# Projection of a hybrid diffusion layer: its token columns in four groups of 428 to 512 instead of six of 304

## The chip, the cores and the metric

The kernel runs on one core of a Trainium2 chip. The metric is the device time of one execution in microseconds (us), the median of the runs. A core has a matmul engine (PE; its weight loads are shown apart as PEld), a vector engine (DVE), a scalar engine (ACT), a general engine (POOL), and SP, which here only issues DMA transfers. Each engine works through its own list of instructions in order, and they meet through semaphores.

## The reference, cut to what matters

One layer of a diffusion model over 1280 tokens (256 context tokens, 1024 latent ones), each with 1024 features, in float32. The part that is changed is the first:

```python
m = jax.nn.silu(cond) @ w_ada + b_ada          # modulation: 6 x 1024 columns, for two conditions
h = rmsnorm(x, gain) * (1.0 + scale) + shift   # adaln
gq, gk, gv, gg, glr, sq, sk, sv = jnp.split(h @ w_in, idx, axis=-1)   # 2848 columns
g_f = heads(jax.nn.log_sigmoid(lr_f @ w_gk_f + b_gk_f) / GATE_TEMP)   # gates, and g_b alike
```

After it come gated linear attention in both directions, windowed attention, the output projection and a squared-ReLU MLP, which the change leaves as they are. The 2848 columns of `w_in` are: 0 to 1023 the queries and keys of the linear attention, 1024 to 1535 its values, 1536 to 2047 an output gate, 2048 to 2079 the low-rank gate input, 2080 to 2847 query, key and value of the windowed attention.

## The kernel before, in words

A product in float32 is made of three matmuls on operands that are split in two, `x = hi + lo`: hi·hi, hi·lo and lo·hi. `project` (L643) computes `h @ w_in`. It goes over the columns of `w_in` in groups (`GROUPS`, L351). Of a token group (columns from 1024 on) the items are the ten tiles of 128 tokens: 24 matmuls each (8 blocks of the contraction, three products), the token tile as the stationary operand and the weight columns, 304 of them, as the moving one. Of a channel group (queries and keys, 256 columns) the items are blocks of 128 columns times three chunks of 512, 512 and 256 tokens: the weights are stationary and the tokens move. That is 84 items in all, numbered n = 0 to 83. All engines run through the same item numbers and do, at fixed numbers, what is due there:

- PE multiplies item n into one of four PSUM banks, after the bank's last item has been copied out (`staged`). At a group's first item it waits for the group's split weights.
- ACT (odd n) or DVE (even n) copies item n to `stage`. SP stores it at position n and waits there until the copy is made (L725 and the line before it), so that everything SP issues later in its list waits too.
- A group's weights are loaded by SP into one of two rooms of `raw` at `FIRST_ITEM[g]` for group g + 1 (L377), split by ACT (high part, L814) and POOL (low part, L868) at item 2 or 3 of group g. The second group alone is split in halves, by DVE and POOL.
- The other two thirds of the modulation weights, 16 slices of 1 MB, use the same rooms after a group is split: SP loads one (L152), PE multiplies it (L188) at an item of `slice_at`, and its room may then be loaded again (`slice_used`).
- The gates (`Gates`, eight blocks, begun every 7 items): PE logits, ACT a softplus of seven instructions with two table loads (L594 to L598), DVE sums and a scan (L609 to L640), SP a store. The heads (`HeadsPrep`, ten tiles, begun every 4.5 items) norm and rotate the windowed queries and keys, in turns between POOL (L446 to L464) and DVE (L471 to L489).
- Near the end SP loads the keys and first tiles of the next stage.

An ACT position is, in order: copy out item n, split, softplus. A DVE position is: copy out item n, low part of a split (if any), modulation, gates, heads.

Of the kernel before, what the change touches and what calls it, by code (L numbers as in the profile page):

```python
# [108 lines left out]
class Modulation:  # L109
# [531 lines left out]
def project(nc, keep, a, raw, hi, lo, scratch, outs, keys, rec, room, stored, mod_out):  # L643
# [4 lines left out]
    with ExitStack() as ctx:  # L648
        s = Space(nc, ctx, "prj")
        whi = [s.sb(f"whi{j}", [P, KD, COLS_IN], F32R) for j in range(2)]  # L650
        wlo = [s.sb(f"wlo{j}", [P, KD, COLS_IN], F32R) for j in range(2)]
# [4 lines left out]
        whi_half, wlo_half, whi_ready, wlo_ready, first_lo_ready, acc_ready = (s.sem(n) for n in (  # L656
            "whi_half", "wlo_half", "whi_ready", "wlo_ready", "first_lo_ready", "acc_ready"))
# [26 lines left out]
        rows_at = {FIRST_ITEM[6]: 1, FIRST_ITEM[9] + 5: 2}  # L684
# [26 lines left out]
        with nc.Block() as block:  # L711
# [152 lines left out]
            def _(pool):  # L864
# [2459 lines left out]
```

## Time and profile before

| | |
|---|---|
| median of 3 runs | 1648.76 us (1645.47 to 1649.05) |
| the profiled execution | 1647.43 us, of which span 1645.7 us |
| mean granted TensorE clock | 0.991 |
| PE busy, share of the span | 1588.2 us, 97% |
| PEld, POOL, DVE, ACT busy | 85%, 62%, 59%, 42% |
| projection: first to last matmul | 40.2 to 388.4 us |

PE is busy in 97% of the span, and no other engine is near it. The page counts overlapping matmuls, so that busy time says nothing about how fast they follow each other: that is to be read from the starts of consecutive matmuls in the timeline. The profile covers one execution; 1.7 us of its time lie outside the span.

### The profile page before, as it was taken

What the parts mean: (1) busy time and instruction counts of PE and PEld (TensorE: products, weight loads), DVE (VectorE), ACT (ScalarE), POOL (GpSimd) and SP (SyncE); (2) the same over time, 40 slices, a digit from 0 to 9 for tenths busy, and PEclk for the clock granted to TensorE, in tenths of its full rate; (3) what the DMA queues carried; (4) which work ended last, traced back from release to release, by engine and by line L of the source; (5) the groups of instructions that cost most, each with busy time, mean ns of one, the idle gap of its engine ahead of it and who ended that gap; (6) DMA issues with size and microseconds to landing.
All of it is one profiled execution on the core that took longest, in us unless ns stands there. A gap on an engine that the chain in (4) does not pass through costs nothing.

```text
span 1645.7 us, 31938 instructions
## 1 busy us (share of the span) xinstructions
PE 1588.2 (97%) x11618; PEld 1391.1 (85%) x11618; DVE 973.5 (59%) x1503; ACT 687.3 (42%) x1212; POOL 1019.1 (62%) x784
## 2 busy tenths in 40 slices
PE   4999999998999999999999999999999999999998
PEld 1999778897788877788889899998979899998987
DVE  2713564775665665457866656666694545545468
ACT  2513323324454566213444444444535444444441
POOL 1711455573485799103777777687898767676673
PEclk7999999999999999999999999999999999999999
DMA  8344555749655763334743132331344132231313
GB/s 323 109 131 165 187 181 191 264 143 257 195 162 171 230 179 114 147 130 155 215 167 103 51 102 63 90 95 58 103 132 150 52 102 73 80 102 51 102 52 115
DMA packets 211450, 225.93 MB, mean 137 GB/s; under 512 B 52752, under 2 KB 171664, under 8 KB 208144
## 3 DMA queue, kind: packets, MB, share of 16 engines
q1 hardware_dynamic: 209248, 224.46, 42.9%
q8 instruction: 70, 1.15, 0.3%
q10 hardware_dynamic: 2096, 0.02, 0.1%
q14 instruction: 36, 0.29, 0.1%
HBM read 177.22 MB, written 47.24 MB: 136 GB/s over the span
## 4 chain that ended last, share of the span: by engine, by line
PE 44%; POOL 4%; DVE 1%; issue 1%; ACT 0%; DMA 0%; SPq 0%; DVEq 0%; ACTq 0%; POOLq 0%
PE ff_banks L3189 8%; PE ff_banks L3190 8%; PE ff_banks L3191 8%; PE ff_banks L3162 7%; PE ff_banks L3164 7%; PE ff_banks L3163 7%; POOL h_whi L2835 1%; POOL h_xop L2432 1%; POOL h_wlo L2847 1%; POOL h_whi L2842 1%; DVE ff_tmp L3036 0%; DMA ff_hb<-in_w_ff 0%; DVE ff_acc L3026 0%; DVE ff_acc L2993 0%; POOL h_wlo L2882 0%
## 5 line engine op out<-in xcount | busy, mean ns | idle before, releaser
L3162 PE MATMUL ff_banks<-h_xop,h_whi 128*128 128x320 f32 x888 | 275.2, 310 | 4.6 <-POOL h_whi L2835 2.0
L3164 PE MATMUL ff_banks<-h_xop,h_whi 128*128 128x320 f32 x888 | 274.4, 309 | 0.0
L3163 PE MATMUL ff_banks<-h_xop,h_whi 128*128 128x320 f32 x888 | 274.3, 309 | 0.0
L2993 DVE TENSOR_TENSOR ff_acc<-ff_acc,ff_banks 128x512 f32<-128x512 f32 x296 | 200.6, 681 | 100.5 <-PE ff_banks L3191 98.9
L3189 PE MATMUL ff_banks<-h_wlo 128*128 128x512 f32 x580 | 226.5, 390 | 1.6 <-POOL h_whi L2842 0.8
L3191 PE MATMUL ff_banks<-h_wlo 128*128 128x512 f32 x580 | 225.6, 389 | 0.0
L2835 POOL TENSOR_TENSOR h_whi<-mid_raw,h_whi 128x512 fp32r<-128x512 f32 x149 | 208.4, 1415 | 1.4 <-ACT h_whi L2687 1.4
L2847 POOL TENSOR_TENSOR h_wlo<-mid_raw,h_wlo 128x320 fp32r<-128x320 f32 x128 | 116.7, 913 | 127.4 <-ACT mid_raw L2724 127.4
L3162 PEld LDWEIGHTS ff_banks<-h_xop,h_whi 128*128 128x128 f32 x888 | 166.7, 188 | 8.3 <-issue 3.6
L3163 PEld LDWEIGHTS ff_banks<-h_xop,h_whi 128*128 128x128 f32 x888 | 166.7, 188 | 1.1
L3164 PEld LDWEIGHTS ff_banks<-h_xop,h_whi 128*128 128x128 f32 x888 | 166.7, 188 | 0.0
L972 PE MATMUL prj_banks<-prj_whi,h_hi 128*128 128x304 f32 x480 | 148.1, 309 | 3.4 <-DVE h_lo L341 2.2
L2835 POOL TENSOR_TENSOR h_whi<-ff_tmp,h_whi 128x512 fp32r<-128x512 f32 x63 | 105.6, 1676 | 67.6 <-ACT h_whi L2687 67.6
L974 PE MATMUL prj_banks<-prj_whi,h_lo 128*128 128x304 f32 x480 | 145.5, 303 | 0.0
L973 PE MATMUL prj_banks<-prj_wlo,h_hi 128*128 128x304 f32 x480 | 144.9, 302 | 0.0
L2687 ACT ACTIVATE h_whi<-mid_raw 128x512 fp32r<-128x512 f32 x149 | 89.9, 623 | 97.7 <-DVE mid_raw L2949 91.4
L3189 PEld LDWEIGHTS ff_banks<-h_wlo 128*128 128x128 f32 x580 | 108.9, 188 | 25.0 <-DVE ff_acc L2993 1.9
L3191 PEld LDWEIGHTS ff_banks<-h_wlo 128*128 128x128 f32 x580 | 108.9, 188 | 23.0
L2717 ACT ACTIVATE mid_raw<-wo_raw 128x320 f32<-128x320 f32 x128 | 60.3, 471 | 159.5 <-DVE wo_raw L2971 65.2
L3190 PE MATMUL ff_banks<-h_whi,h_wlo 128*128 128x512 f32 x310 | 120.7, 389 | 0.0
L3190 PE MATMUL ff_banks<-h_wlo 128*128 128x512 f32 x290 | 113.1, 390 | 0.0
L825 ACT ACTIVATE prj_stage<-prj_banks 128x304 f32<-128x304 f32 (+2 forms) x47 | 21.0, 446 | 220.5 <-PE prj_banks L974 133.7
(323 smaller groups left out, 3771.6 us busy)
## 6 DMA issues: line engine op xcount, KB each, us to landing
mid_raw<-in_w_ff SPq DMA_DIRECT2D x124, 512.0 KB, 4.4
mid_raw<-in_w_ada SPq DMA_DIRECT2D x18, 1024.0 KB, 7.2
early_room<-qk_by_channel SPq DMA_DIRECT2D x20, 512.0 KB, 4.2
proj<-prj_stage SPq DMA_DIRECT2D x60, 152.0 KB, 1.9
mid_raw<-in_w_in SPq DMA_DIRECT2D x6, 1216.0 KB, 7.3
early_room<-in_w_ada SPq DMA_DIRECT2D x6, 1024.0 KB, 11.1
decays<-early_room SPq DMA_DIRECT2D x8, 640.0 KB, 4.6
early_room<-decays SPq DMA_DIRECT2D x20, 256.0 KB, 2.9
```

Source lines behind the costliest of these rows:

```text
L972: pe.matmul(out, x_hi, whi[j][:, k, 0:w], start=(k == 0), stop=False)
L973: pe.matmul(out, x_hi, wlo[j][:, k, 0:w], start=False, stop=False)
L974: mm = pe.matmul(out, x_lo, whi[j][:, k, 0:w], start=False, stop=(k == KD - 1))
L2835: pool.tensor_tensor(lo, source(q, i), hi.bitcast(F32), ALU.subtract).then_inc(w1lo_ready, 1)
L2847: pool.tensor_tensor(ulo[j][c][:, t0:t0 + TH], v[i % 2], uhi[j][c][:, t0:t0 + TH].bitcast(F32), ALU.subtract).then_inc(ulo_ready, 1)
L2993: dve.tensor_tensor(acc[:, p, at], acc[:, p, at], down[n % RING], ALU.add).then_inc(added, 1)
L3162: pe.matmul(out, w_hi[:, k], x_hi[:, k], start=(k == 0), stop=False)
L3163: pe.matmul(out, w_hi[:, k], x_lo[:, k], start=False, stop=False)
L3164: mm = pe.matmul(out, w_lo[:, k], x_hi[:, k], start=False, stop=(k == KH - 1))
L3189: pe.matmul(out, x_hi, w_hi[c][:, at], start=(c == 0), stop=False)
L3190: pe.matmul(out, x_hi, w_lo[c][:, at], start=False, stop=False)
L3191: mm = pe.matmul(out, x_lo, w_hi[c][:, at], start=False, stop=(c == 1))
```

## The change

Token columns come in groups of 428, 428, 512 and 456 (1824 as before); the channel columns in groups of 256, 256, 128, 128 and 256. Group order: 428, 256, 428, 256, 512, 128, 128, 256, 456. There are 64 items instead of 84: 40 token items and the same 24 channel items; the groups begin at items 0, 10, 16, 26, 32, 42, 45, 48 and 54 (before: 0, 10, 20, 30, 36, 42, 48, 54, 64 and 74). The two rooms of `raw` get different sizes (8 x 512 and 8 x 256 words); `raw` and the split buffers grow by 15 KB per partition together, and a scratch area of the DMA is cut to 1024 bytes. All groups after the first are split in halves of the contraction: ACT makes both high halves, DVE the first low half and POOL the second. The numbers at which loads, splits, slices, gates and heads are due are written out as tables, in part closer together: gates now every 4 or 5 items and heads every 3 or 4, and two of a gate's steps on DVE one item earlier. The last group is loaded at item 47 and split by ACT at item 48, and slices are multiplied after items 49, 51 and 53.

The diff, cut to its core:

```diff
-GROUPS = ((1936, 304), (2240, 304), (2544, 304), (0, 256), (256, 256), (512, 256), (768, 256), (1024, 304), (1328, 304), (1632, 304))
+GROUPS = ((1992, 428), (0, 256), (2420, 428), (256, 256), (1024, 512), (512, 128), (640, 128), (768, 256), (1536, 456))
 NG = len(GROUPS)
-COLS_IN = max(w for _, w in GROUPS)
+COLS_IN = [max(w for _, w in GROUPS[j::2]) for j in range(2)]
+RAW_IN = [0, KD * COLS_IN[0], KD * sum(COLS_IN)]
 QK = 2 * GW
...
+def raw_group(raw, g):
+
+    at = RAW_IN[g % 2]
+    return raw[:, at:at + KD * GROUPS[g][1]].rearrange("p (k n) -> p k n", k=KD)
+
+
+def load_group(eng, a, raw, g):
     at, w = GROUPS[g]
-    return eng.dma_start(raw[:, j, :, 0:w], a["w_in"][0].rearrange("(k p) n -> p k n", p=P)[:, :, at:at + w])
+    return eng.dma_start(raw_group(raw, g), a["w_in"][0].rearrange("(k p) n -> p k n", p=P)[:, :, at:at + w])
...
-        turn_at = {FIRST_ITEM[1] + 5 + 2 * c: c for c in range(len(CHUNKS))}
-        gate_at = {FIRST_ITEM[2] + 7 * n: n for n in range(H)}
-        heads_at = {FIRST_ITEM[3] + 3 + 9 * t // 2: t for t in range(NT)}
-        assert max(gate_at) + 8 < LAST and max(heads_at) + 6 < LAST
-
-
-        slices = [(g, at) for g, places in ((2, (3, 7)), (3, (2, 5)), (4, (2, 5)), (5, (2, 5)), (6, (5,)), (7, (2, 5, 9)), (8, (1, 5, 9)), (9, (4,))) for at in places]
-        slice_at = {FIRST_ITEM[g] + at: i for i, (g, at) in enumerate(slices)}
-        slice_load_at = {}
-        for i, (g, at) in enumerate(slices):
-            same = i and slices[i - 1][0] == g
-            slice_load_at[FIRST_ITEM[g] + (slices[i - 1][1] + 1 if same else 0 if g < 7 else -1 if g == 7 else -3)] = i
+        turn_at = {15: 0, 17: 1, 19: 2}
+        gate_at = {20: 0, 24: 1, 29: 2, 33: 3, 38: 4, 42: 5, 47: 6, 51: 7}
+        heads_at = {22: 0, 25: 1, 29: 2, 33: 3, 36: 4, 40: 5, 43: 6, 47: 7, 51: 8, 54: 9}
+        load_at = {10: 2, 16: 3, 26: 4, 32: 5, 42: 6, 43: 7, 47: 8}
+        high_at = {12: 2, 19: 3, 28: 4, 35: 5, 42: 6, 44: 7, 48: 8}
+        low_at = [{13: 2, 21: 3, 29: 4, 36: 5, 42: 6, 45: 7, 50: 8}, {13: 2, 20: 3, 28: 4, 36: 5, 42: 6, 45: 7, 49: 8}]
+        TAIL = 60
+        assert len(ITEMS) == 64 and max(gate_at) + 6 < TAIL and max(heads_at) + 4 < TAIL
+
+
+        slices = [(2, 21), (2, 23), (2, 25), (3, 27), (3, 29), (4, 33), (4, 35), (4, 37), (4, 41), (5, 42), (7, 49), (7, 51), (7, 53), (8, 54), (8, 56), (8, 58)]
+        slice_at = {at: i for i, (g, at) in enumerate(slices)}
+        slice_load_at = {at: i for i, at in enumerate((17, 22, 24, 25, 28, 32, 34, 36, 38, 40, 48, 50, 52, 53, 55, 57))}
...
-        rows_at = {FIRST_ITEM[6]: 1, FIRST_ITEM[9] + 5: 2}
-        cols_at = {FIRST_ITEM[6] + 1: 1, FIRST_ITEM[9] + 6: 2}
-        pick_at = {FIRST_ITEM[6] + 2: 1, FIRST_ITEM[9] + 7: 2}
-        assert len(slices) == 2 * KD and slices[KD - 1][0] == 5 and slices[KD] == (6, 5)
+        rows_at = {38: 1, 59: 2}
+        cols_at = {39: 1, 60: 2}
+        pick_at = {40: 1, 61: 2}
+        assert len(slices) == 2 * KD and all(FIRST_ITEM[g] <= at < FIRST_ITEM[g + 1] for g, at in slices)
...
+        def half_of(g, half):
+
+            ks = slice(half * KH, (half + 1) * KH)
+            return raw_group(raw, g)[:, ks], wide(whi, g)[:, ks], wide(wlo, g)[:, ks]
+
+        def split_until(eng, g):
+
+            if g == 0:
+                eng.wait_ge(first_lo_ready, 1)
+            else:
+                for half in range(2):
+                    eng.wait_ge(wlo_ready[half], g)
+
+        def low_half(eng, g, half):
+
+            src, hi_out, lo_out = half_of(g, half)
+            eng.wait_ge(whi_ready[half], g)
+            eng.tensor_tensor(lo_out, src, hi_out.bitcast(F32), ALU.subtract).then_inc(wlo_ready[half], 1)
         def width(n):
...
-                    if n == FIRST_ITEM[g] and 1 <= g < NG - 1:
-                        if g == 1:
-                            sp.wait_ge(first_lo_ready, 1)
-                        else:
-                            sp.wait_ge(wlo_ready, g - 1)
-                        if used_until[g - 1]:
-                            sp.wait_ge(ada.slice_used, KD + used_until[g - 1])
-                        load_group(sp, a, raw, g + 1, (g + 1) % 2).then_inc(w_in[(g + 1) % 2], 16)
+                    if n in load_at:
+                        g = load_at[n]
+                        split_until(sp, g - 2)
+                        if used_until[g - 2]:
+                            sp.wait_ge(ada.slice_used, KD + used_until[g - 2])
+                        load_group(sp, a, raw, g).then_inc(w_in[g % 2], 16)
                     if n in slice_load_at:
                         i = slice_load_at[n]
                         room = slices[i][0]
-                        sp.wait_ge(wlo_ready, room)
-                        sp.wait_ge(ada.slice_used, KD + (i if room == g else used_until[room - 2]))
+                        split_until(sp, room)
+                        sp.wait_ge(ada.slice_used, KD + (i if slices[i - 1][0] == room else used_until[room - 2]))
...
-                    if n - 8 in gate_at:
-                        gates.sp_store(sp, gate_at[n - 8])
-                    if n == FIRST_ITEM[9]:
-                        sp.wait_ge(ada.slice_used, KD + used_until[8])
+                    if n - 6 in gate_at:
+                        gates.sp_store(sp, gate_at[n - 6])
+                    if n == FIRST_ITEM[NG - 1]:
+                        split_until(sp, NG - 1)
+                        sp.wait_ge(ada.slice_used, KD + used_until[NG - 2])
                         keys.sp_load_cache(sp)
-                    if n == max(heads_at) + 6:
-                        sp.wait_ge(ada.slice_used, 3 * KD)
+                    if n == TAIL:
                         for j in range(2):
...
+                def high_half(g, half):
+                    src, hi_out, lo_out = half_of(g, half)
+                    act.wait_ge(w_in[g % 2], 16 * (g // 2 + 1))
                     if g >= 2:
                         act.wait_ge(acc_ready, FIRST_ITEM[g - 1])
-                    act.activation(whi[j][:, :, cols], raw[:, j, :, cols], ACT.Copy).then_inc(whi_ready, 1)
-
-                def split_second(half):
-                    cols, ks = split_slices(1), slice(half * KH, (half + 1) * KH)
-                    act.wait_ge(w_in[1], 16)
-                    act.activation(whi[1][:, ks, cols], raw[:, 1, ks, cols], ACT.Copy).then_inc((whi_half, whi_ready)[half], 1)
+                    act.activation(hi_out, src, ACT.Copy).then_inc(whi_ready[half], 1)
...
-                    if n == FIRST_ITEM[g] + (2 if by_channel(g) else 3) and 1 <= g < NG - 1:
-                        split(g + 1)
+                    if n in high_at:
+                        for half in range(2):
+                            high_half(high_at[n], half)
...
-                    if n == FIRST_ITEM[g] + (2 if by_channel(g) else 3) and 1 <= g < NG - 1:
-                        split(g + 1)
+                        low_half(pool, 1, 1)
+                    if n in low_at[1]:
...
+                    if n in low_at[0]:
+                        low_half(dve, low_at[0][n], 0)
...
+                    if n - 3 in gate_at:
+                        gates.dve_gate(dve, gate_at[n - 3])
                     if n - 4 in gate_at:
-                        gates.dve_gate(dve, gate_at[n - 4])
+                        gates.dve_scan(dve, gate_at[n - 4])
                     if n - 5 in gate_at:
-                        gates.dve_scan(dve, gate_at[n - 5])
-                    if n - 6 in gate_at:
-                        gates.dve_relative(dve, gate_at[n - 6])
+                        gates.dve_relative(dve, gate_at[n - 5])
...
-        wide, late = PAST // P * KV * 2 * DH, NT * KV * 2 * DH
-        self.kc = flat[:, 0:wide].rearrange("p (b k c d) -> p b k c d", k=KV, c=2, d=DH)
-        self.k = flat[:, wide:wide + late].rearrange("p (t k c d) -> p t k c d", k=KV, c=2, d=DH)
+        at, late, wide = 4 * HALF, NT * KV * 2 * DH, PAST // P * KV * 2 * DH
+        self.k = raw[:, at:at + late].rearrange("p (t k c d) -> p t k c d", k=KV, c=2, d=DH)
+        self.kc = raw[:, at + late:at + late + wide].rearrange("p (b k c d) -> p b k c d", k=KV, c=2, d=DH)
...
-    nc = bacc.Bacc("TRN2", target_bir_lowering=False, num_devices=1)
+    nc = bacc.Bacc("TRN2", target_bir_lowering=False, num_devices=1, dynamic_dma_scratch_size=1024)
```

## Rows read from the trace of the kernel before

**Rows 1.** Waits of PE from 40 to 388.3 us, then busy time of 60 to 390:

```profile
PE prj_banks L972 <- DVE h_lo L341: 2.2, 1, 2.2
PE prj_banks L972 <- POOL h_lo L341: 1.2, 1, 1.2
PE prj_banks L188 <- DMA mid_raw<-in_w_ada: 0.3, 1, 0.3
...
60.00:390.00 330.00, 328.04 (x2125) 294.09 (x2123) 167.91 (x206) 98.21 (x121) 143.81 (x89) 1.00 0.56 176
```

**Rows 2.** Timeline of PE: start, duration, line; two matmuls 24 apart, two 15 apart:

```profile
100.01 0.30 PE L972 MATMUL prj_banks<-prj_whi,h_hi 128*128 128x304 f32 x1
...
103.35 0.30 PE L972 MATMUL prj_banks<-prj_whi,h_hi 128*128 128x304 f32 x1
...
160.02 0.40 PE L982 MATMUL prj_banks<-h_hi,prj_whi 128*128 128x512 f32 x1
...
163.50 0.39 PE L982 MATMUL prj_banks<-h_hi,prj_whi 128*128 128x512 f32 x1
```

**Rows 3.** Timeline of the start, and the window 22 to 34 us:

```profile
34.45 1.94 PE L188 MATMUL prj_banks<-mid_raw,prj_ada_silu 128*32 128x512 f32 x8
...
40.23 0.59 PE L972 MATMUL prj_banks<-prj_whi,h_hi 128*128 128x304 f32 x1 [2.24 <-DVE h_lo L341]
...
22.00:34.00 12.00, 5.95 (x31) 1.69 (x32) 4.96 (x4) 3.85 (x7) 4.00 (x6) 0.64 1.02 411
```

**Rows 4.** Timeline of DVE and POOL, 293 to 305 us, and a scan:

```profile
293.70 0.83 DVE L478 SCALAR_TENSOR_TENSOR prj_xn<-early_room,prj_rstd 128x640 f32<-128x640 f32 x1 [0.26 <-POOL prj_rstd L452]
...
296.39 2.35 POOL L464 TENSOR_TENSOR prj_sq<-prj_xg,prj_rope 128x320 f32<-128x320 f32 x2
298.70 5.40 POOL L868 TENSOR_TENSOR prj_wlo<-mid_raw,prj_whi 128x2432 fp32r<-128x2432 f32 x1
...
298.83 5.96 DVE L489 TENSOR_TENSOR prj_xr<-prj_xc,prj_sq 128x640 f32<-128x640 f32 x1 [1.66 <-POOL prj_sq L464]
...
339.85 2.83 DVE L621 TENSOR_TENSOR_SCAN early_room<-early_room 128x1290 f32<-128x1290 bf16 x1
```

**Rows 5.** Timeline of PE: a slice, and the matmul behind it:

```profile
299.36 1.06 PE L188 MATMUL prj_banks<-mid_raw,prj_ada_silu 128*32 128x512 f32 x8 [0.33 <-DMA mid_raw<-in_w_ada]
300.36 0.41 PE L972 MATMUL prj_banks<-prj_whi,h_hi 128*128 128x304 f32 x1
```

**Rows 6.** SP at 269 us, and landing of 512 KB in the page:

```profile
269.22 0.70 SPq L236 DMA_DIRECT2D mod_rows<-prj_ada_rows  x2
...
271.40 1.12 SPq L163 DMA_DIRECT2D prj_ada_rows<-in_b_ada  x4
...
mid_raw<-in_w_ff SPq DMA_DIRECT2D x124, 512.0 KB, 4.4
```

**Rows 7.** DMA issues: size and us to landing, at 277 and 293 us:

```profile
mid_raw<-in_w_in SPq DMA_DIRECT2D x1, 1216.0 KB, 8.1
mid_raw<-in_w_ada SPq DMA_DIRECT2D x1, 1024.0 KB, 5.4
...
mid_raw<-in_w_ada SPq DMA_DIRECT2D x1, 1024.0 KB, 6.7
```

**Rows 8.** Timeline of ACT: half a split, and first and last of a softplus:

```profile
58.67 1.21 ACT L819 ACTIVATE prj_whi<-mid_raw 128x1216 fp32r<-128x1216 f32 x1
...
314.93 1.63 ACT L594 ACTIVATE early_room<-prj_banks,prj_bgk 128x512 f32<-128x512 f32 x3
...
320.46 1.27 ACT L598 ACTIVATE early_room<-early_room 128x1280 f32<-128x1280 f32 x1
```

**Rows 9.** Windows: PE, PEld, DVE, ACT, POOL busy, clock, DMA share, GB/s:

```profile
388.00:390.50 2.50, 0.36 (x3) 0.11 (x1) 0.00 (x0) 0.42 (x1) 0.00 (x0) 1.00 1.04 400
...
392.00:395.00 3.00, 3.00 (x16) 2.67 (x14) 2.29 (x3) 2.49 (x5) 2.96 (x4) 0.50 1.22 302
...
400.00:418.00 18.00, 13.27 (x184) 10.67 (x184) 15.48 (x28) 9.48 (x19) 9.98 (x13) 0.93 0.92 264
```

More of the change, by code:

```diff
@@ L649, in project @@
         s = Space(nc, ctx, "prj")
-        whi = [s.sb(f"whi{j}", [P, KD, COLS_IN], F32R) for j in range(2)]
-        wlo = [s.sb(f"wlo{j}", [P, KD, COLS_IN], F32R) for j in range(2)]
+        whi = [s.sb(f"whi{j}", [P, KD, COLS_IN[j]], F32R) for j in range(2)]
+        wlo = [s.sb(f"wlo{j}", [P, KD, COLS_IN[j]], F32R) for j in range(2)]
         stage = s.sb("stage", [P, RING, HALF])
@@ L655, in project @@
         w_in = [s.sem(f"w_in{j}") for j in range(2)]
-        whi_half, wlo_half, whi_ready, wlo_ready, first_lo_ready, acc_ready = (s.sem(n) for n in (
-            "whi_half", "wlo_half", "whi_ready", "wlo_ready", "first_lo_ready", "acc_ready"))
+        first_hi_ready, first_lo_ready, acc_ready = (s.sem(n) for n in ("first_hi_ready", "first_lo_ready", "acc_ready"))
+        whi_ready, wlo_ready = ([s.sem(f"{n}{half}") for half in range(2)] for n in ("whi_ready", "wlo_ready"))
         staged = [s.sem("staged_dve"), s.sem("staged_act")]
@@ L695, in staged_value, with wide @@
             return staged[on_act(n)], sum(1 for m in range(n + 1) if on_act(m) == on_act(n))
-        def split_slices(g):
-            return slice(0, GROUPS[g][1])
+        def wide(w, g):
+            return w[g % 2][:, :, 0:GROUPS[g][1]]
+        def half_of(g, half):
[11 more added lines that the diff above has]
+            eng.tensor_tensor(lo_out, src, hi_out.bitcast(F32), ALU.subtract).then_inc(wlo_ready[half], 1)
         def width(n):
@@ L804, in _ @@
                         if t + 2 < NT:
+                            wait_stored(FIRST_ITEM[2] + t + 3)
                             prep.sp_load(sp, t + 2)
@@ L808, in _, with first_high @@
             def _(act):
[L809 to L811 removed]
+                def first_high():
+                    act.wait_ge(w_in[0], 16)
+                    act.activation(wide(whi, 0), raw_group(raw, 0), ACT.Copy).then_inc(first_hi_ready, 1)
+                def high_half(g, half):
+                    src, hi_out, lo_out = half_of(g, half)
+                    act.wait_ge(w_in[g % 2], 16 * (g // 2 + 1))
                     if g >= 2:
                         act.wait_ge(acc_ready, FIRST_ITEM[g - 1])
[L814 to L819 removed]
+                    act.activation(hi_out, src, ACT.Copy).then_inc(whi_ready[half], 1)
                 def evacuate(n):
@@ L829, in _ @@
                 ada.act_exp(act)
-                split(0)
+                first_high()
                 for t in range(norm.XR):
@@ L864, in _ @@
             def _(pool):
-                def split(g):
-                    j, cols = g % 2, split_slices(g)
-                    pool.wait_ge(whi_ready, g + 1)
-                    pool.tensor_tensor(wlo[j][:, :, cols], raw[:, j, :, cols], hi_view(whi[j])[:, :, cols], ALU.subtract).then_inc(wlo_ready, 1)
-                def split_second(pool):
-                    cols, ks = split_slices(1), slice(KH, KD)
-                    pool.wait_ge(whi_ready, 2)
-                    pool.wait_ge(wlo_half, 1)
-                    pool.tensor_tensor(wlo[1][:, ks, cols], raw[:, 1, ks, cols], hi_view(whi[1])[:, ks, cols], ALU.subtract).then_inc(wlo_ready, 1)
                 norm.pool_constants(pool)
@@ L927, in _ @@
                     if n == NT - 1:
-                        cols, ks = split_slices(1), slice(0, KH)
-                        dve.wait_ge(whi_half, 1)
-                        dve.tensor_tensor(wlo[1][:, ks, cols], raw[:, 1, ks, cols], hi_view(whi[1])[:, ks, cols], ALU.subtract).then_inc(wlo_half, 1)
+                        low_half(dve, 1, 0)
+                    if n in low_at[0]:
+                        low_half(dve, low_at[0][n], 0)
                     if n == NT:
@@ L3283, in build @@
             sm = Space(nc, outer, "mid")
-            raw = sm.sb("raw", [P, 2, KD, COLS_IN], side="right")
+            raw = sm.sb("raw", [P, RAW_IN[2]], side="right")
             keys = Keys(sm, a, scratch, raw)
```

37 lines of the change are left out of this document (12 added, 25 removed).

## The prediction

> **What bounds the kernel now.** I read the waits of PE first. In the whole projection PE waits three times, 3.7 us together, and from 60 to 390 us it is busy for 328.04 of 330, the rest being the change of stage at 388.4; its clock is 1.00 [rows 1]. So PE sets the end of this stage, and an edit gains only what it takes from PE's own list, while a wait that is added there counts in full. Second I read the pitch of matmuls from their starts [rows 2]: 24 of 304 columns take 3.34 us, 139 ns each; 15 of 512 take 3.48 us, 232 ns each. The line through both is 0.447 ns a column and 3.3 ns a matmul.
>
> **Fewer, wider matmuls.** The columns stay; 60 token items become 40, so 480 matmuls go, at 3.3 ns: **-1.6 us**. The starts are rounded to 10 ns, so the pitches are good to 0.5 ns and the intercept lies between 2 and 5 ns: -1.0 to -2.4.
> The Trainium skill ("TensorE: Matmul & The Clock Gate", section Back-to-back issue gap) says that in a stream of weight loads and matmuls the sustained spacing is about 81 ns at 128 columns and 131 ns at 512. By that a matmul would carry 64 ns that do not depend on its columns, and the sum would get -31 us from this part. The rows, 232 ns at 512, speak against it.
>
> **The start.** The first group is 124 columns wider, 496 KB (0.51 MB) more in front of the last modulation slices. DMA is full there, share 1.02 and 411 GB/s, and the last slice's matmuls begin at 34.45, the first product at 40.23 through a chain of DVE and ACT [rows 3]: 0.51 MB / 411 GB/s = **+1.2 us** (0 if the last slice had slack, 1.6 at the most). Longer first items cover PE's second wait, for a low part by POOL, 1.2 us [rows 1]: **-1.2 us** (0 to -1.2).
>
> **The next groups.** I go through the tables in the same way for each group: when SP can issue the load, 5.4 to 8.1 us to landing, two high halves, two low halves, PE's need. Groups 2, 3 and 5 come out split 8 us or more ahead of PE, group 4, the one of 512 columns, about 2, and slices 0 to 9 are there 1 us or more ahead; I take 0 (0 to +1). The half splits cost ACT little more than the whole ones and take half of POOL's 5.40 us; DVE and POOL exclude each other in such work, as the xr sum shows that took 5.96 us beside POOL's split, against 0.83 for the like xn [rows 4]. No PE time hangs on this until item 42.
>
> **Group 6, due at item 45.** Let item 42 start at 0. Items 42, 43, 44 take 5.6, 5.6 and 2.8 us, logits 0.6, a slice 1.0 [rows 5]: PE comes to item 45 at 15.6. SP stores the modulation rows first and loads the next bias, 269.22 to 272.52 = 3.3 us [rows 6], so the load goes out at 3.9; 512 KB land 4.4 later, at 8.3. A high half of 512 elements is 0.6, DVE's low half 0.65: 9.6. Behind that low half on DVE stand a scan, 2.83, and the heads' xn, and POOL waits for this xn: from xn to the end of xs 293.70 to 298.74 = 5.0 us [rows 4]. Only then POOL comes to its low half, 512 elements at 2.2 ns (5.40 us / 2432): 1.2. Sum 18.6, 3 us late. The chain may save a us on landing and overlap; I take **+2 us** (0 to +3).
>
> **Group 7, due at item 48.** From item 45 PE needs 5.6 + 5.6 + 2.8 + 0.6 = 14.6. POOL's list from there: the heads' square 1.3, shut out by DVE's xr and rel for some 3.5; DVE's sum 0.8, copy 0.4, negatives 1.8, low half 1.2, gate 1.5; xn to xs 5.0; POOL's low half, 1024 elements, 2.3: 17.8. **+3 us** (0 to +4). With 304-column groups this chain had 20 items more of time.
>
> **The last group and slice 11: the largest term.** Let item 48 start at 0. PE wants slice 11 behind item 51 and its logits: 5.6 + 5.6 + 1.0 + 2.8 + 5.6 + 0.6 = 21.2. The load of group 8 is issued at item 47, when DVE has copied out item 46: at -2.5 if DVE is on time, at +2.4 if it is held in the heads chain as above; I take +1. It is 1824 KB, with 1024 KB of slice 10 and smaller ones right behind. 1216 KB beside another 1024 KB took 8.1 us to land [rows 7]; 3.7 MB at 411 GB/s and 2 us on top are 11. It lands at +12 (+5.6 to +13.4). ACT has stood since 0 in front of this split, at item 48. Then two halves of 1824 elements at 1.0 ns (1.21 us / 1216): 3.4; then, in its list, the softplus of gate 6, 314.93 to 321.73 = 6.8 us [rows 8]; and only then it copies out item 49, which SP has to store before it issues slice 11: 0.6 + 0.9. Slice 11 takes 5.4 to 6.7 us to land [rows 7]. Sum 12 + 3.4 + 6.8 + 1.5 + 6 = 29.7 against 21.2: PE waits 8.5; with what the terms can give, **+7.5 us**. The bounds: with all the best ones 5.6 + 3.4 + 6.8 + 1.5 + 5.4 = 22.7, +1.5; with all the worst 13.4 + 3.4 + 6.8 + 1.5 + 6.7 = 31.8, +10.6. Slices 12 to 15 then follow two items of 8.4 to 10 us apart: +0.5 (0 to +1.5).
>
> **The clock.** After the 2.2 us in which PE stood at 388.4 to 390.6 the granted clock was 0.50 from 392 to 395, at 1.2 instead of 2.4 GHz [rows 9], which over 3.4 us costs 1.7. The wait of 0.33 us [rows 5] brought nothing like it. I count one such dip, behind the longest wait: **+1.7 us** (0 to three dips, 5).
>
> **The end.** Copies of the keys and first tiles are issued at item 60, where three items, 15 us, are left: as before or a little earlier. From 400 to 418 PE is busy in 13.27 of 18 us with DMA at 0.92 [rows 9]; less traffic left over could give back 0 to 3, since most of it is issued there. I take 0. Buffer addresses and the smaller scratch area touch no row that I can find: 0.
>
> **Sum.** -1.6 + 1.2 - 1.2 + 0 + 2 + 3 + 7.5 + 0.5 + 1.7 = **+13.1**. It is made against the profiled execution, 1647.43 us, 1.3 below the median of the runs, inside their spread: **1660.5 us**. Its own range: from +5 to +20, 1652.5 to 1667.5.
>
> **Rivals.**
> - *The waits are short.* DVE is on time at item 46, so group 8 is issued at -2.5 and lands early: -1.6 + 1.2 - 1.2 and only 1.5 to 5 at slice 11, with or without a dip: 0 to +5, say 1650. For it: DVE is busy in only 59% of the span. Against: in the sum for group 7 its steps stand back to back with those of POOL, with none to spare. Chance 0.16.
> - *Nothing waits: the tables have slack enough.* Slices landed within 5.4 us, and before the change PE waited only 0.3 us for one of sixteen. Then -1.6 remains, 1645.8. Against it stands that ACT's own list, 3.4 + 6.8, plus two landings one behind the other, is longer than four items. Chance 0.12.
> - *The other side, faster: the next stage starts better.* One mechanism: the keys and first tiles are in before the stage changes, and of the 4.7 us that PE idles from 400 to 418 [rows 9] 3 come back, while slice 11 is on time; it decides from a wait below 1.5 us there. -1.6 - 3 = 1642.8. Against it: the loads that are late there are issued after 400. Chance 0.06.
> - *Weight loads set the spacing,* so that fewer matmuls give much more: by the pitches [rows 2] a fixed part above 5 ns is excluded for these shapes, unless 428 and 456 columns behave unlike both. With 20 ns each -9.6 and the waits +14.7: 1652.5. Chance 0.03. The rule of the Trainium skill's page above, with 64 ns, would be this rival at its largest; the trace does not agree.
> The forecast has 0.63.
>
> **How the numbers follow.** A change within 0.2%, 3.3 us around 1648.8, cannot be told from none. Faster: the third rival, 0.06, and 0.03 from the second. Same: the rest of the second, 0.09, most of the first, 0.10, and 0.01 of the last. Slower: 0.71. The range for 8 in 10 reaches from the second rival's upper half to the forecast's worst terms but one: 1646.5 to 1667.
>
> **What would show it.** Right: PE waits on the split's low part at items 45 and 48 for 1 to 4 us; one wait on `mid_raw<-in_w_ada` of 5 to 9 us behind item 51; ACT idle for about 10 us until `in_w_in` lands, and its copy of item 49 some 7 us after PE is done with it; a pitch of 194 to 195 ns at 428 columns; a granted clock of 0.5 for 3.4 us behind the long wait. Wrong: ACT free at item 49, slice 11 landing ahead of PE, or an end of the projection earlier than 388 us.

## The result, and the profile of the changed kernel

The change makes the kernel slower: 1654.77 us median of 15 runs (1651.25 to 1662.36) against 1647.57 us for the kernel before. The ratio is 1.0054, 95% interval 1.0041 to 1.0066: 8.9 us, between 7 and 11. The medians are 7.2 us apart; one of the 15 runs of the kernel before took 3292.3 us, and without it they are 8.2 us apart. The profiled execution took 1658.27 us with a span of 1656.5, 10.8 us more than the profiled one of before; it is 3.5 us above its kernel's median, so what is read from it is the loss of that execution. The forecast, +13.1 us, had the direction, was some 4 us above the 8.9 us of the ratio, and had its largest term in the wrong place.

Waits of PE in the changed kernel, 38 to 400 us (total, times, longest), in answer to [rows 1]:

```profile
PE prj_banks L188 <- DMA mid_raw<-in_w_ada: 5.7, 4, 2.3
PE prj_banks L991 <- issue: 4.0, 2, 2.3
PE mix_st L1489 <- PEq L95: 2.4, 1, 2.4
PE prj_banks L981 <- DVE h_lo L341: 2.2, 1, 2.2
```

The 1.2 us behind POOL's `h_lo` are gone; 4.0 us stand in front of split weights (`issue` here: the page names no releaser, but L991 is the first matmul of a group), and 5.7 us at slices, where [rows 1] had 0.3. The timeline of PE places each (start, duration, line; in brackets the idle time before it):

```profile
41.34 0.43 PE L981 MATMUL prj_banks<-prj_whi,h_hi 128*128 128x428 f32 x1 [2.23 <-DVE h_lo L341]
...
218.29 1.07 PE L188 MATMUL prj_banks<-mid_raw,prj_ada_silu 128*32 128x512 f32 x8 [0.25 <-DMA mid_raw<-in_w_ada]
285.11 0.47 PE L991 MATMUL prj_banks<-h_hi,prj_whi 128*128 128x512 f32 x1 [1.64 <-issue]
302.05 0.47 PE L991 MATMUL prj_banks<-h_hi,prj_whi 128*128 128x512 f32 x1 [2.32 <-issue]
316.62 1.06 PE L188 MATMUL prj_banks<-mid_raw,prj_ada_silu 128*32 128x512 f32 x8 [1.78 <-DMA mid_raw<-in_w_ada]
328.19 1.07 PE L188 MATMUL prj_banks<-mid_raw,prj_ada_silu 128*32 128x512 f32 x8 [1.38 <-DMA mid_raw<-in_w_ada]
357.46 1.94 PE L188 MATMUL prj_banks<-mid_raw,prj_ada_silu 128*32 128x512 f32 x8 [2.28 <-DMA mid_raw<-in_w_ada]
399.29 1.06 PE L1489 MATMUL mix_st<-keep_mats,mid_raw 128*128 128x128 f32 x8 [2.36 <-PEq L95]
...
673.58 1.06 PE L2233 MATMUL mix_gla<-keep_mats,mid_raw 128*128 128x128 f32 x8 [2.03 <-DMA mid_raw<-mix]
```

They are, in order, the first product, a slice of group 4, items 45 and 48, slices 10, 11 and 14, and the first matmul of the next stage, which before began at 390.59: +8.70. The last row is no part of the projection: there PE waits for the mixing stage's output, and before it waited there for nothing. Around it stand two matmuls that are the same in both kernels, first before, then after; between them the difference grows from 6.4 to 10.6 us:

```profile
660.60 0.32 PE L1861 MATMUL mix_score<-keep_mats,mix_peak 128*100 128x128 f32 x1 [1.07 <-DVE mix_peak L2112]
675.64 1.07 PE L2366 MATMUL ff_banks<-keep_mats,mid_raw 128*128 128x128 f32 x8 [1.22 <-PEq L95]
```

```profile
667.01 0.32 PE L1866 MATMUL mix_score<-keep_mats,mix_peak 128*100 128x128 f32 x1 [1.33 <-DVE mix_peak L2117]
686.27 1.06 PE L2371 MATMUL ff_banks<-keep_mats,mid_raw 128*128 128x128 f32 x8 [1.23 <-PEq L95]
```

Windows at half clock, in answer to [rows 9] (PE, PEld, DVE, ACT, POOL busy; clock; DMA share; GB/s):

```profile
302.00:306.00 4.00, 3.95 (x11) 3.20 (x12) 4.00 (x3) 0.00 (x0) 1.25 (x1) 0.60 0.45 108
357.00:361.00 4.00, 3.54 (x13) 1.71 (x14) 2.18 (x3) 0.00 (x0) 1.68 (x2) 0.57 0.28 71
675.00:681.00 6.00, 5.14 (x35) 4.21 (x32) 2.23 (x5) 1.26 (x3) 1.23 (x2) 0.50 0.14 51
```

Each follows one of the waits above, and the last stretch is 6.8 us long. POOL's low halves of groups 6 and 7 end at 285.00 and 301.94, 0.11 us ahead of PE's first matmul of items 45 and 48:

```profile
283.74 1.26 POOL L724 TENSOR_TENSOR prj_wlo<-mid_raw,prj_whi 128x512 fp32r<-128x512 f32 x1
299.61 2.33 POOL L724 TENSOR_TENSOR prj_wlo<-mid_raw,prj_whi 128x1024 fp32r<-128x1024 f32 x1
```

Last the pitch, the time from the start of one matmul to the start of the next: 21 matmuls of 428 columns take 4.12 us, 196 ns each (predicted 194 to 195).

```profile
64.97 0.36 PE L982 MATMUL prj_banks<-prj_wlo,h_hi 128*128 128x428 f32 x1
...
69.09 0.36 PE L982 MATMUL prj_banks<-prj_wlo,h_hi 128*128 128x428 f32 x1
```

### The profile page after: what moved, and what is told of

It is laid out like the page before. It is cut to its first block, busy times and chain, and to the rows that moved or that the text cites. A ratio compares the mean times of both kernels' runs of the same rounds, so it can differ in the third digit from the quotient of the medians.

```text
span 1656.5 us, 30950 instructions
## 1 busy us (share of the span) xinstructions
PE 1589.8 (96%) x11138; PEld 1371.2 (83%) x11138; DVE 972.5 (59%) x1500; ACT 687.1 (41%) x1208; POOL 995.0 (60%) x783
## 4 chain that ended last, share of the span: by engine, by line
PE 45%; POOL 4%; DVE 1%; issue 0%; ACT 0%; DMA 0%; SPq 0%; POOLq 0%; ACTq 0%
PE ff_banks L3194 8%; PE ff_banks L3195 8%; PE ff_banks L3196 8%; PE ff_banks L3167 7%; PE ff_banks L3169 7%; PE ff_banks L3168 7%; POOL h_whi L2840 1%; POOL h_xop L2437 1%; POOL h_wlo L2852 1%; POOL h_whi L2847 1%; PE ff_banks L3209 1%; PE ff_banks L3211 1%; PE ff_banks L3210 1%; DMA ff_hb<-in_w_ff 0%; POOL h_wlo L2887 0%
## 5 line engine op out<-in xcount | busy, mean ns | idle before, releaser
L981 PE MATMUL prj_banks<-prj_whi,h_hi 128*128 128x428 f32 (+2 forms) x320 | 120.1, 375 | 2.2 <-DVE h_lo L341 2.2
L983 PE MATMUL prj_banks<-prj_whi,h_lo 128*128 128x428 f32 (+2 forms) x320 | 118.5, 370 | 0.0
L982 PE MATMUL prj_banks<-prj_wlo,h_hi 128*128 128x428 f32 (+2 forms) x320 | 118.3, 370 | 0.0
L847 ACT ACTIVATE prj_stage<-prj_banks 128x428 f32<-128x428 f32 (+3 forms) x37 | 19.9, 537 | 201.5 <-PE prj_banks L983 149.1
```

What stands on the lines that cost most here:

```text
L981: pe.matmul(out, x_hi, whi[j][:, k, 0:w], start=(k == 0), stop=False)
L982: pe.matmul(out, x_hi, wlo[j][:, k, 0:w], start=False, stop=False)
L983: mm = pe.matmul(out, x_lo, whi[j][:, k, 0:w], start=False, stop=(k == KD - 1))
```

## Experiments

Ratios are to the kernel before, of runs on the same chip. Below, "theory" and a letter are the explanations that each expectation sets against each other. The last column is the start of the next stage in the profiled execution, 390.59 before.

| kernel | ratio | 95% interval | next stage at |
|---|---|---|---|
| changed | 1.0054 | 1.0041 to 1.0066 | 399.29 |
| e1 lows on DVE | 1.0050 | 1.0034 to 1.0067 | 398.49 |
| e2 load 8 early | 1.0031 | 1.0018 to 1.0043 | 394.11 |
| e3 split 8 later | 1.0046 | 1.0031 to 1.0061 | 395.24 |
| e5 three edits | 1.0019 | 1.0008 to 1.0030 | 390.68 |
| e9 = e1, heads apart | 1.0020 | 1.0008 to 1.0031 | 391.68 |
| e8 = e5, heads apart | 1.0004 | 0.9995 to 1.0013 | 388.17 |
| e7 before, small scratch | 0.9997 | 0.9988 to 1.0006 | 390.46 |
| e10 = e8, more code | 0.9992 | 0.9981 to 1.0004 | 389.17 |
| e11 before, more code | 1.0009 | 0.9999 to 1.0020 | 390.95 |
| e12 changed, more code | 1.0051 | 1.0035 to 1.0068 | 400.23 |

**e1: do the waits at items 45 and 48 hang on POOL's low half?**

```diff
-                    if n in low_at[1]:
+                    if n in low_at[1] and low_at[1][n] not in (6, 7):
                         low_half(pool, low_at[1][n], 1)
...
                         low_half(dve, low_at[0][n], 0)
+                        if low_at[0][n] in (6, 7):
+                            low_half(dve, low_at[0][n], 1)
```

> The changed kernel, but VectorE makes both low halves of groups 6 and 7 (512 and 1024 elements more), GpSimd none of them. Theory A (each added wait of PE counts with its own cause): the waits of 1.64 us at item 45 and 2.32 us at item 48 had GpSimd's low half behind the heads' chain; both go below 0.5 us. Half of the 4.0 us comes back at slices 10 and 11, whose loads don't move with PE, so 1.5 to 3 us less than the changed kernel, a ratio to before of 1.0036 to 1.0045. Theory B (these waits come from the late landing of the loads, not from the order on GpSimd): the waits stay above 1.2 and 1.8 us, ratio 1.0054. Theory C (the added time is clock, not waits): ratio 1.0054, while the waits go.

Both waits went, so PE had stood for POOL's low half, which POOL reached only behind its steps for the heads (the row of 299.61 above follows them without a gap). In e12, the changed kernel with more code, the profile names POOL as what item 45 waited for:

```profile
285.91 0.47 PE L991 MATMUL prj_banks<-h_hi,prj_whi 128*128 128x512 f32 x1 [1.90 <-POOL prj_wlo L724]
```

But PE's wait at slice 10 grew by 4.8 us, from 1.78 to 6.61. The waits of the projection sum to 8.3 us, 9.65 in the changed kernel, where half of 4.0 was expected to go: the ratio hardly moved. Timeline of DVE, SP and PE in e1:

```profile
302.39 0.82 DVE L496 TENSOR_TENSOR prj_xr<-prj_xc,prj_sq 128x640 f32<-128x640 f32 x1 [1.66 <-POOL prj_sq L471]
303.13 0.68 DVE L915 COPY prj_stage<-prj_banks 128x512 f32<-128x512 f32 x1
...
304.32 0.44 SPq L384 DMA_DIRECT2D mid_raw<-in_w_in  x1
306.72 0.56 SPq L152 DMA_DIRECT2D mid_raw<-in_w_ada  x1
...
317.19 1.93 PE L188 MATMUL prj_banks<-mid_raw,prj_ada_silu 128*32 128x512 f32 x8 [6.61 <-DMA mid_raw<-in_w_ada]
```

DVE copies item 46 only behind its last step for the heads (`prj_xr`); SP stores that item, loads group 8, then slice 10. In the changed kernel the same three stand at 302.55, 303.74 and 306.07. The chain of the heads on DVE and POOL holds all of it, and PE, 4 us earlier, waits for it at the next place.

**e2: group 8's load two items earlier.**

```diff
-        load_at = {10: 2, 16: 3, 26: 4, 32: 5, 42: 6, 43: 7, 47: 8}
+        load_at = {10: 2, 16: 3, 26: 4, 32: 5, 42: 6, 43: 7, 45: 8}
```

> The changed kernel, with the load of group 8 (1824 KB) issued at SP's item 45, not 47, thus some 15 us earlier and ahead of slice 10 by a whole landing. Theory A (slices 10 and 11 were late because that load shared the queue with slice 10 and held ScalarE at item 48, its copy of item 49 and so SP): no idle of ScalarE at item 48, slice 10 lands in 5 to 6.5 us and not in 10.5, the waits of 1.78 and 1.38 us go, those at items 45 and 48 stay: 3.2 us and the granted-clock dip behind item 48 as before, ratio 1.0032 to 1.0038. Rival (slices 10 and 11 are late by the queue of SP, which issues them only behind their items' copies): both waits stay within 0.5 us, ratio 1.0050 to 1.0056.

Slices 10 and 11 no longer wait; 1.71 and 2.32 us at items 45 and 48 stay, and 1.76 at slice 14. The 1824 KB in front of slice 10, issued at 303.74 in the changed kernel and 293.70 here, made both late. The ratio is 1.0031, at the lower end of the 1.0032 to 1.0038 that were expected.

**e3: ACT's split of group 8 at item 50.**

```diff
-        high_at = {12: 2, 19: 3, 28: 4, 35: 5, 42: 6, 44: 7, 48: 8}
+        high_at = {12: 2, 19: 3, 28: 4, 35: 5, 42: 6, 44: 7, 50: 8}
```

(and both `low_at` of group 8 at 51)

> The changed kernel, with ScalarE's split of group 8 at its item 50 instead of 48 and both low halves at item 51: ScalarE doesn't stand idle for the load and copies out item 49 at once. The load and slice 10 stay where they are. Theory A, its ScalarE half: slice 11 is issued right behind slice 10's matmuls, at about 318 and not 322.75, and its wait of 1.38 us goes; slice 10's wait of 1.78 us stays: ratio 1.0044 to 1.0048. Rival (the DMA traffic alone made both late): both waits stay, ratio 1.0054.

As theory A has it: slice 11's wait of 1.38 us went, slice 10's stayed at 1.55, ratio 1.0046. So ACT's stand at item 48 cost slice 11, the traffic slice 10. Sizes of this order lie inside the interval; the trace, not the ratio, tells them apart.

**e5: three edits together** (those of e1 and e2, and slices 14 and 15 one item later):

```diff
-  ... (8, 54), (8, 56), (8, 58)]
+  ... (8, 54), (8, 57), (8, 59)]
```

> The changed kernel with three edits together: both low halves of groups 6 and 7 on VectorE, the load of group 8 at item 45, and slices 14 and 15 used at items 57 and 59 instead of 56 and 58 (load of slice 15 at item 58, the second pick's steps one item later). Theory A: of 9.65 us of added waits in the projection at most 2 remain, in slices 10 and 13, and 480 fewer matmuls give their 2 us: the end of the projection at 387 to 390 us against 390.6 before, ratio 0.9985 to 1.0005. Theory C (clock or something behind the projection carries the added time): ratio above 1.003 although the waits are gone. Rival D (a wait taken away comes back one item on): the waits sum to 5 us or more, ratio 1.0025 or more.

In the trace 1.70 us at slice 10 and 0.23 at slice 13 are left and the projection ends where it did before: the waits were the loss. The ratio, 1.0019, is above the 0.9985 to 1.0005 of theory A. The trace shows two things that can make it so, not how much each is worth: the wait for the mixing output is here too (1.44 us), and the first product comes at 42.35.

**e9 and e8: the heads' chain itself.**

```diff
-        heads_at = {22: 0, 25: 1, 29: 2, 33: 3, 36: 4, 40: 5, 43: 6, 47: 7, 51: 8, 54: 9}
+        heads_at = {22: 0, 25: 1, 29: 2, 33: 3, 36: 4, 39: 5, 44: 6, 47: 7, 51: 8, 54: 9}
```

> As e1 (both low halves of groups 6 and 7 on VectorE), with the heads' steps of tiles 5 and 6 begun at items 39 and 44 instead of 40 and 43. In e1 slice 10 was issued at 306.72, because VectorE copied item 46 out at 303, behind its steps for the heads of tile 6, and SP stores that item and the heads before it issues slice 10; PE, 4 us earlier, then waited 6.6 us. Theory A2 (one chain of heads' steps on VectorE and GpSimd holds the copy of item 46, SP, the load of group 8 and slice 10): the copy and both loads go out 4 us or more earlier, slice 10's wait goes from 6.6 to below 1 us, 0 to 3 us appear at slice 11, end of the projection at 389 to 394 us, ratio 1.001 to 1.003. Rival (slice 10 is late by its own landing beside 1824 KB, or PE's wait moves on whatever is done): slice 10 and 11 together still wait 5 us or more, ratio 1.0045 or more.

The timeline of DVE, SP and PE in e9:

```profile
294.83 0.69 DVE L915 COPY prj_stage<-prj_banks 128x512 f32<-128x512 f32 x1 [1.75 <-PE prj_banks L995]
...
296.02 0.44 SPq L384 DMA_DIRECT2D mid_raw<-in_w_in  x1
298.58 0.43 SPq L152 DMA_DIRECT2D mid_raw<-in_w_ada  x1
...
321.98 1.93 PE L188 MATMUL prj_banks<-mid_raw,prj_ada_silu 128*32 128x512 f32 x8 [2.69 <-DMA mid_raw<-in_w_ada]
351.40 1.06 PE L188 MATMUL prj_banks<-mid_raw,prj_ada_silu 128*32 128x512 f32 x8 [1.05 <-DMA mid_raw<-in_w_ada]
```

DVE waits for PE now, not PE for DVE. Copy and loads are 8 us earlier, 6.61 us at slice 10 became none, and 2.69 appeared at slice 11, as expected. Two numbers in a table are worth 6.8 us at the projection's end and 0.3% of the time. Of the 6.8, 4.5 are waits (8.3 to 3.7 us), some 1.7 a stretch at half clock that is 3.4 and not 6.8 us long, and 0.4 an earlier start.

> As e5 (VectorE's lows, load of group 8 at item 45, slices 14 and 15 later), with the heads' steps of tiles 5 and 6 at items 39 and 44 and slice 13 used at item 55 instead of 54. Theory A2: e5's waits of 1.70 us (slice 10) and 0.23 us go, none above 0.7 us is left in the projection; the end comes 2 us before that of e5, at 387 to 389 us; with the start 1 to 2 us late and some 2.5 us fewer by the matmuls, and the 1.4 us at the mixing output's load as in e5: ratio 0.9995 to 1.0012, e5's 1.0019 less 0.0010. Rival (what is left over before is the half clock and the later stages, and this edit only moves a wait): ratio 1.0017 to 1.0030.

e8 (with slice 13 at item 55 too) has one wait of 0.97 us left besides one of 0.28 and ends the projection at 388.17, 2.4 us ahead of before. With 1.0004 it is not faster: its first product comes at 41.70, and behind the projection PE waits 2.39 us for the mixing output.

**e7: the scratch area alone.**

```diff
-    nc = bacc.Bacc("TRN2", target_bir_lowering=False, num_devices=1)
+    nc = bacc.Bacc("TRN2", target_bir_lowering=False, num_devices=1, dynamic_dma_scratch_size=1024)
```

> The kernel before, with one part of the change alone: the scratch area for dynamic DMA cut to 1024 bytes. All five executions of changed kernels wait 1.4 to 2.5 us at 664 to 674 us for a load of the mixing output, before did not, and all its stores there land later (3.0 to 3.4 us in the middle against 2.2). Theory S (the smaller scratch area makes that wait): the wait is here too, ratio 1.0008 to 1.002. Theory N (the prediction's 0 for the scratch area; that wait hangs on when the stores fall, and comes and goes from one execution to the next): ratio 0.9993 to 1.0007, whatever this execution shows there.

Theory N for the scratch area: 0.9997, and no wait at the mixing output. But it was not chance either: that wait, 0.3 to 2.5 us, is in the profile of every kernel tried so far that has the changed projection, and in neither of the two with the old one. The activity of the DMA engines from the last store of the mixing stage to the load behind it tells more. First e5, 652.7 to 656.7 us, then before, 654.9 to 657.2 (40 slices each; busy tenths, GB/s, queues):

```profile
DMA  0003999999999899930000001010100010000000
GB/s 0 0 0 143 348 389 389 410 369 348 349 389 451 328 492 369 369 103 0 0 0 0 0 0 20 0 20 0 20 0 20 20 41 20 0 0 0 0 0 0
q1 hardware_dynamic: 288, 0.52, 35.8%
q8 instruction: 1, 0.02, 1.6%
```

```profile
DMA  0000006979999999969969969979963700000000
q1 hardware_dynamic: 288, 0.52, 59.9%
q14 instruction: 1, 0.01, 1.6%
```

The same 288 packets. In e5 one packet of 16 KB of `q8 instruction` is among them. (`q14 instruction`, 8 KB, is in the window of before, whose store landed in time.) The bulk is through at 1.8 us of the window, and from 2.4 to 3.4 us packets follow singly at 20 GB/s: they look like those behind that one on one engine. SP waits for the last, and issues the next loads 4.1 us after the store, 2.4 before.

**e10, e11, e12: shift the transfers of code.** TensorE's program has 960 instructions fewer, and `q8 instruction` fell from 70 packets to 66, while `q14 instruction` stayed at 36; so `q8` brings TensorE's code.

```diff
                 for n, (g, m, b) in enumerate(ITEMS):
+                    for _ in range(8 if 12 <= n < 60 else 0):
+                        pe.wait_ge(mats_in, 16)
```

(two such waits make one instruction: 192 more; e11 has 64 more in the kernel before, `2 if 14 <= n < 78`)

> As e8, with 192 instructions more in TensorE's program between items 12 and 60: waits on a semaphore that has long been there, 4 instructions an item. The changed program has 960 TensorE instructions fewer than before (480 matmuls with their weight loads) and 4 of 70 transfers of code fewer, so one transfer of code holds some 256 instructions and each falls in another place of the later stages; 192 more put them where before had them, less three whole transfers. Theory F (the wait of 1.4 to 2.5 us at the mixing output's load comes from a 16 KB transfer of code that falls between the stores of the mixing stage, whose last then lands 1.7 us later): the store at 652 us lands in 2 us, the loads behind it are issued 2.4 us and not 4.1 us after it, the wait goes below 0.4 us, and the ratio is 0.9985 to 0.9998, faster than before and than e8 (1.0004). Rival (the placement of the code has nothing to do with it): issue after 4.1 us, the wait stays, ratio 1.0000 to 1.0012.

> The kernel before with 64 instructions more in TensorE's program (one satisfied wait instruction at each of the items 14 to 77), which puts the transfers of code where the changed kernel has them in the later stages (960 fewer is 64 more, less four whole transfers of 256). Theory F: the loads at 657 us are issued 4.1 us and not 2.4 us after the last store, and PE waits 1.2 us or more for the mixing output, without any other part of the change; ratio 1.0006 to 1.0020. Rival (something else in the change makes that wait): it doesn't appear, ratio 0.9995 to 1.0005.

> The changed kernel with the same 192 instructions more as in e10. Theory F: of its 1.0054 the part behind the projection goes (1.4 to 2.5 us of wait and in most executions a stretch at half clock of 3.4 to 6.8 us behind it, 1.7 to 3.4 us): ratio 1.0025 to 1.0042, with the five waits of the projection as they were. Rival: 1.0048 to 1.0060.

SP and PE in e10, then in e11:

```profile
651.03 0.43 SPq L1068 DMA_DIRECT2D mix<-mix_glo_out  x1
653.42 0.81 SPq L2263 DMA_DIRECT2D mid_raw<-in_x_sample  x2
```

```profile
651.99 0.43 SPq L1060 DMA_DIRECT2D mix<-mix_glo_out  x1
656.09 0.81 SPq L2256 DMA_DIRECT2D mid_raw<-in_x_sample  x2
...
664.15 1.06 PE L2230 MATMUL mix_gla<-keep_mats,mid_raw 128*128 128x128 f32 x8 [1.82 <-DMA mid_raw<-mix]
```

Theory F in both directions: 64 satisfied waits put the 4.1 us and a wait of 1.82 us into the kernel before, and 192 take them out of e8 (2.4 us, no wait, span 1642.0 against 1646.5). In e12 the wait is gone too. All thirteen profiles agree: in the eight in which such a packet falls among those of the store (changed, e1, e2, e3, e5, e8, e9, e11) SP issues the next load 4.0 to 4.3 us after it, in the other five (before, e6, e7, e10, e12) 2.4 to 2.5. What that costs PE is less regular: it waits 2.53 us in e3 and 0.29 in e9, and 1.30 in e6 (the last experiment), where the store landed in time and the packet came behind it. The ratios agree in sign (e10 is 0.0012 below e8, e11 0.0012 above e7), but each interval touches its neighbour, and that of e10 holds 1, so it is not shown to beat the kernel before. The mechanism is shown by the traces; its price in the median is not. For e12 the expected fall to 1.0025 to 1.0042 didn't come: its projection waited differently (4.84 us at slice 10) and began 0.6 us later.

**e6: what a matmul costs beside its columns.** Each matmul of group 8 as two of 228 columns.

```diff
+                        cuts = (0, w // 2, w) if n >= FIRST_ITEM[NG - 1] else (0, w)
+                        for a, b in zip(cuts, cuts[1:]):
+                            pe.matmul(out[:, a:b], x_hi, whi[j][:, k, a:b], start=(k == 0 and a == 0), stop=False)
...
```

> The changed kernel, with every token matmul of the last group (456 columns) made as two of 228 columns: 240 matmuls more, the same columns. By the line of the prediction (0.447 ns a column and 3.3 ns a matmul) the pitch at 228 columns is 105 ns, an item of 48 takes 5.06 us instead of 4.98, and the ten together 0.8 us more. Rival (weight loads or issue carry a fixed part that wider matmuls hide): a pitch of 120 ns or more, 3.6 us or more for the ten items.

It was executed once, so it has no ratio.

```profile
341.60 0.28 PE L983 MATMUL prj_banks<-prj_whi,h_hi 128*128 128x228 f32 x1
...
344.28 0.27 PE L983 MATMUL prj_banks<-prj_whi,h_hi 128*128 128x228 f32 x1
```

24 take 2.68 us, 112 ns each: between the two pitches expected. At 456 columns it is 208.5 ns, so halving adds 15 ns a matmul, not 3.3, and 3.6 us to the ten items. That is the rival's 3.6 us, but not its 120 ns: with 480 such matmuls 120 ns would have added 7.6 us, so its two figures did not belong together. The line of the prediction holds from 256 to 512 columns within 5 ns and is 7 ns off at 228.

## Why the prediction came out as it did

The working is in the order of the prediction's terms; measured values are those of the profiled execution and add up to its 10.8 us.

| step | predicted | measured |
|---|---|---|
| fewer, wider matmuls | -1.6 | -2.7 |
| start | +1.2 | +1.1 |
| POOL's low part covered | -1.2 | -1.2 |
| next groups, slices 0 to 9 | 0 | +0.25 |
| group 6, item 45 | +2 | +1.64 |
| group 7, item 48 | +3 | +2.32 |
| slices 10 and 11 | 0 and +7.5 | +1.78 and +1.38 |
| slices 12 to 15 | +0.5 | +2.28 |
| half clock in the projection | +1.7 | two stretches, +3.2 |
| half clock at the start, before only | none | -1.2 |
| a slice's wait of before, change of stage | 0 | -0.2 |
| behind the projection | 0 | +2.1 |

**Right:** PE's list as the bound, the pitch, that POOL's wait goes, and both waits for split weights, with mechanism and size (e1). The estimate from the Trainium skill ("TensorE: Matmul & The Clock Gate", section Back-to-back issue gap), a gain of 31 us, is not borne out: the pitch is 196 ns at 428 columns. The -2.7 is what the balance of +8.70 leaves. The pitches give the same within 0.2: some -2.0 for the token items and -0.8 for the channel items, whose pitch at 512 columns was 228 ns, 231 before; why is open.

**In part luck.** The start met its +1.2 in this execution. Over all profiles the first product comes at 40.0 to 40.2 us in the three with the old groups and at 40.8 to 42.5, mean 41.7, in the ten with the new ones: +1.6, the prediction's worst case. And the total is only 2.3 us off the 10.8 of the profiled executions because terms that were too high by 8.0 us together (slices 10 and 11 by 4.3 of them) stand against terms that were too low by 5.6.

**The step that failed: slice 11, +7.5.** Its chain is there link by link, but PE waits 1.38 us there and not 8.5: the slice comes 3.6 us earlier than predicted, and PE 3.6 us later. With item 48 at 0 the load was issued at +1.7 (+1 assumed), landed at +9.7 (+12): 1824 KB took 8.0 us, as 1216 KB had (8.1, [rows 7]), not 11. The traffic I had added to it fell on slice 10, which was issued 2.3 us later and took 10.5 us. ACT's part was as predicted [rows 8]; its timeline has the idle 12.18 us, the split's 3.34, the softplus, and the copy of item 49 behind them:

```profile
311.74 3.34 ACT L841 ACTIVATE prj_whi<-mid_raw 128x1824 fp32r<-128x1824 f32 x2 [12.18 <-DMA mid_raw<-in_w_in]
314.99 1.61 ACT L599 ACTIVATE early_room<-prj_banks,prj_bgk 128x512 f32<-128x512 f32 x3
...
320.50 1.28 ACT L603 ACTIVATE early_room<-early_room 128x1280 f32<-128x1280 f32 x1
321.68 0.58 ACT L847 ACTIVATE prj_stage<-prj_banks 128x512 f32<-128x512 f32 x1
```

Slice 11 was issued at 322.75 and there at 328.19, +26.1 where 29.7 were predicted. On the other side PE came at +24.8, not +21.2: it had lost 1.78 us at slice 10, where I had put no wait, and 1.6 at half clock. The sign that I had named, one wait of 5 to 9 us behind item 51, did not show. What delays PE ahead of a late transfer is taken off that transfer's wait. Together the two slices and the clock between them cost 4.8 us for 9.2 predicted.

**The sum treated as separate what hangs on one chain.** Items 45 and 48, group 8's load and slice 10 all stand behind the heads' steps that DVE and POOL pass to and fro. I had that chain with its price [rows 4], but used it twice as a wait of its own, and in the load's issue only as a range. e1 shows the price of that view, e9 the right one: taking out waits of 4.0 us moved the projection's end by 0.8 us (1.9, if one allows for a start 1.1 us later), and moving the chain moved it by 6.8 more.

**Slice 14** waits 2.28 us and exceeds the bound of its term (+1.5): it is issued at 349.60, an item and its copies behind slice 13, and landed 7.9 us later, not 5.4 to 6.7 [rows 7]. e5, e8 and e10, which give it an item more, have no wait there.

**The missing term: code.** "Buffer addresses and the smaller scratch area touch no row" was right for the scratch area (e7). What I overlooked is that 960 instructions fewer move the later transfers of code. One met the stores at 661 us: 1.7 us later landing, 2.03 us of wait, and a stretch at half clock behind it, together 4.2 us in this execution (e5 and e11 have waits of 1.44 and 1.82 us there and no such stretch). The 2.1 in the table is this less 2.3 us that the mixing stage took back, most of it because before had a stretch at half clock at 392 us [rows 9] and the changed kernel none there.

**The clock.** Two stretches in the projection, not one, both behind waits of 2.3 us. The profiled execution of before had one at the start, 40.9 to 44 us, and that of the changed kernel none: executions differ in this. But little was lost by it. e7, with the same projection and no such stretch, begins 0.2 us earlier, waits for POOL's low part not once but twice, and comes to the second place 0.2 us earlier. First before (a window, clock 0.58, the third number from the right; then its one wait), then e7:

```profile
41.00:44.00 3.00, 3.00 (x16) 2.98 (x15) 2.85 (x10) 0.67 (x3) 0.00 (x0) 0.58 0.97 339
...
56.72 0.41 PE L972 MATMUL prj_banks<-prj_whi,h_hi 128*128 128x304 f32 x1 [1.15 <-POOL h_lo L341]
```

```profile
45.75 0.41 PE L972 MATMUL prj_banks<-prj_whi,h_hi 128*128 128x304 f32 x1 [1.19 <-POOL h_lo L341]
...
56.51 0.41 PE L972 MATMUL prj_banks<-prj_whi,h_hi 128*128 128x304 f32 x1 [1.17 <-POOL h_lo L341]
```

So the stretch took 1.2 us of PE's time, the -1.2 of the table, and hid a wait of as much. Longer first items take away both waits: the change gains 2.4 us there against an execution at full clock, twice the predicted 1.2.

The rivals: "the waits are short" named an early landing of group 8, and it came early, but by a shorter transfer; the early issue on which that rival rests did not come (+1.7, not -2.5), nor did its sum of 0 to +5; "nothing waits" is excluded by 9.65 us of waits, "weight loads set the spacing" by the pitches at 428 and 456 columns. "The next stage starts better" did not decide: the gain up to 427 us was 1.8, about what the stretch of before at 392 us costs.

## What to carry to other kernels

When a sum has several waits, first ask which share a chain: two engines that hand steps to and fro, with a queue in program order behind them, are one term, and taking one wait out shows only the next. Such a chain is moved in the table that starts it (here two items of `heads_at`), and a large transfer (here 1824 KB among slices of 1024) is issued well before the small urgent ones, not right in front of them. And fewer instructions are not only less work: they shift the moments at which code is loaded.

## What the runs showed of the hardware

- Code is loaded through the same DMA engines as data, some 240 TensorE instructions to a 16 KB packet (4 packets fewer for 960 instructions fewer, and in e6 2 more for 480 more). In the eight profiles with one such packet among the 288 of a store, the next load went out 4.0 to 4.3 us after it, in the five without 2.4 to 2.5. That it shares one of the 16 engines with the late packets is inferred from their 20 GB/s, not shown.
- Matmuls in this form follow each other by 112 ns at 228 columns, 117 to 120 at 256, 139 at 304, 195 to 196 at 428, 209 at 456, 228 to 232 at 512.
- In these profiles the granted clock was 0.50 behind each of eight waits of PE in the projection of 2.28 us or more, for 3.4 us, and for 6.8 in and behind those of 4.84 and 6.61; behind waits of 1.55 to 1.92 us once in thirteen. The length of a wait alone does not decide it: behind the 2.23 to 2.36 us at the change of stage it fell in four profiles of ten (before, e2, e7, e12) and not in that of the changed kernel. A stretch of 3.4 us costs 1.6 to 1.7: the first 24 matmuls of item 48 were 303 ns apart on the mean, 227 to 233 in items of the same shape at full clock.
- With the new groups the first product came at 40.8 to 41.7 us in the five profiles with a clock of 0.99 to 1.00 from 22 to 34 us, and at 41.9 to 42.5 in the five with 0.50. With the old groups it came at 40.0 to 40.2, at 0.64 (before, e7) and at 0.50 (e11).
